# Attention in a two-layer hybrid block: the weighted values directly behind the next step's scores

## What is computed

```python
def block_attention(q, k, v):                      # 8 query heads, 2 key/value heads, HEAD_DIM 64
    qb = q.reshape(B, nb, Q_BLOCK, N_KV_HEADS, Q_PER_KV, HEAD_DIM).transpose(1, 0, 2, 3, 4, 5)
    def one_block(qblk):
        s = jnp.einsum('bqkgd,bskd->bkgqs', qblk, k, preferred_element_type=jnp.float32) * scale
        p = jax.nn.softmax(s, axis=-1).astype(v.dtype)
        return jnp.einsum('bkgqs,bskd->bqkgd', p, v)
```

## Time and profile before

| | us | share of the span |
|---|---|---|
| profiled execution | 1708.01 | |
| its span | 1706.2 | |
| TensorE matmul busy | 1616.7 | 95% |
| TensorE weight load busy | 1317.9 | 77% |
| VectorE (DVE) busy | 1014.3 | 59% |
| GpSimd (POOL) busy | 877.0 | 51% |
| ScalarE (ACT) busy | 624.3 | 37% |
| median of the three runs | 1710.27 | |

### The profile page before, as it was taken

How to read it: one execution, slowest core, us unless ns; L and a number is a source line. 1 busy time by engine, 2 the same in 40 slices (tenths; PEclk the granted TensorE clock), 3 DMA queues, 4 the chain that set the end, 5 groups by cost and what they waited for, 6 DMA issues and landing times. The chain is left out here.

```text
span 1706.2 us, 39559 instructions
## 1 busy us (share of the span) xinstructions
PE 1616.7 (95%) x17052; PEld 1317.9 (77%) x17052; DVE 1014.3 (59%) x1509; ACT 624.3 (37%) x1262; POOL 877.0 (51%) x763
## 2 busy tenths in 40 slices
PE   5999999989998899999999999998999889999998
PEld 4888999979997555546889999997899754554586
DVE  4563243828774778888338514382777478888911
ACT  5211231124444455555234223112444445545501
POOL 1001489039991477784230047911999338777432
PEclk9999999999999999999999999999999999999999
DMA  9455202210000000122320211221000000010422
GB/s 351 157 173 183 69 27 90 81 62 17 16 5 13 13 13 27 35 77 98 127 100 25 65 39 51 71 95 61 22 17 5 12 14 7 27 40 26 150 98 76
DMA packets 70124, 112.39 MB, mean 66 GB/s; under 512 B 10032, under 2 KB 42176, under 8 KB 69952
## 3 DMA queue, kind: packets, MB, share of 16 engines
q1 hardware_dynamic: 69200, 109.62, 19.3%
q10 hardware_dynamic: 752, 0.25, 0.1%
HBM read 90.30 MB, written 19.47 MB: 64 GB/s over the span
## 5 line engine op out<-in xcount | busy, mean ns | idle before, releaser
L1744 POOL TENSOR_TENSOR attn_accp<-attn_accp,attn_pr 128x1024 f32<-128x1024 f32 x110 | 266.8, 2426 | 48.5 <-ACT attn_pr L1821 43.3
L94 PE MATMUL ps<-in_h_hi,in_w_hi 128*128 128x384 f32 x672 | 226.8, 337 | 0.0
L96 PE MATMUL ps<-in_h_hi,in_w_lo 128*128 128x384 f32 x672 | 225.8, 336 | 0.0
L1821 ACT ACTIVATE attn_pr<-ps 128x512 f32<-128x512 f32 x292 | 158.9, 595 | 170.2 <-PE ps L1981 161.3
L2019 DVE TENSOR_REDUCE attn_mx<-ps 128x1 f32<-128x1152 f32 x128 | 172.3, 1354 | 74.3 <-PE ps L1936 73.5
L1980 PEld LDWEIGHTS ps<-attn_QH,attn_KH 128*128 128x128 f32 x292 | 55.5, 190 | 124.7 <-ACT attn_pr L1821 62.7
L1990 PE MATMUL ps<-attn_pr,z 128*64 128x512 f32 x520 | 140.6, 619 | 0.0
L1224 POOL TENSOR_TENSOR delta_ML<-delta_EK,local 128x256 f32<-128x256 f32 x180 | 130.7, 747 | 14.9 <-PE ps L1264 14.2
L1980 PE MATMUL ps<-attn_QH,attn_KH 128*128 128x512 f32 x292 | 131.8, 451 | 1.6 <-issue 1.4
L94 PEld LDWEIGHTS ps<-in_h_hi,in_w_hi 128*128 128x128 f32 x672 | 126.1, 188 | 5.0 <-issue 5.0
L96 PEld LDWEIGHTS ps<-in_h_hi,in_w_lo 128*128 128x128 f32 x672 | 126.1, 188 | 0.0
(11 more groups left out here) (313 smaller groups left out, 3853.9 us busy)
## 6 DMA issues: line engine op xcount, KB each, us to landing
in_w<-in_w_in SPq DMA_DIRECT2D x21, 1024.0 KB, 5.6
z<-in_w_mod SPq DMA_DIRECT2D x8, 2048.0 KB, 8.2
gates<-in_gate SPq DMA_DIRECT2D x48, 192.0 KB, 1.9
attn_gt<-gates SPq DMA_DIRECT2D x34, 256.0 KB, 2.6
z<-in_x_sample SPq DMA_DIRECT2D x16, 512.0 KB, 6.3
zz<-in_w_mod SPq DMA_DIRECT2D x8, 1024.0 KB, 10.1
out_w<-in_w_out SPq DMA_DIRECT2D x16, 512.0 KB, 6.6
out_y<-z SPq DMA_DIRECT2D x16, 512.0 KB, 2.9
```

Source lines behind the costliest of these rows:

```text
L94: nc.tensor.matmul(out, a_hi(i), b_hi(i), start=(i == 0), stop=False)
L96: last = nc.tensor.matmul(out, a_lo(i), b_hi(i), start=False, stop=(i == n - 1))
L1744: nc.gpsimd.tensor_tensor(acc, a, pr[:, n % 4], ALU.add).then_inc(pool_added, 1)
L1821: nc.scalar.activation(pr[:, n % 4, e], ps[:, e, :], ACT.Exp, scale=HD ** -0.5).then_inc(p_done, 1)
```

## The change

Inside an iteration the values move from the end to the place directly behind the scores. Nothing else is changed.

```diff
         for n, items in enumerate(steps):
             if n + 1 < len(ATTN_STEPS):
                 scores(n + 1)
+            weighted_values(n)
             for item in items:
                 work(item)
-            weighted_values(n)
         out["tensor"](pe, lambda: work(("sum", len(PAIRS) - 1)), nxt)
```

## The result

The changed kernel takes 1722.62 us, the median of 5 runs (1720.39 to 1727.70), against 1710.27 before (of five runs as well, 1708.93 to 1712.72). The ratio is 1.0072, with an interval of 1.0058 to 1.0086: slower by 9.9 to 14.7 us. In the profiled executions the span grew from 1706.2 to 1718.6, by 12.4.

The account below looks back on a forecast made before the run. TensorE, busy for 95% of the span, was taken to bound the kernel. The terms summed to +3.25 us per layer, +6.5 for two, on 1710.3: 1716.8 us, range 1712.5 to 1721, chance 0.70.

Parts of the forecast that it names:

- my third rival: Longer stillness before pair 2's scores drops the clock, up to 3 us more per layer: +12.5, 1723 us; chance 0.08.
- Waits for maxima: TensorE's waits for DVE, nearly all in steps 3 and 15, mostly remain: -0.2 us per layer, bounds -2.1 and 0.
- My first rival: The moved values fill TensorE's waits for maxima, winning 2.1 us per layer: 1709 us in total; chance 0.10.
- Lone sums: Five steps per layer where a maximum parts sum from values: 0.33 us lost each, +1.65, bounds 0 and 1.85.
- Row of pair 2: Values no longer lie under the row's DMA before pair 2's scores: +1.05 us per layer, bounds 0.7 and 1.2.
- Row of the last pair: One of two values blocks leaves the gap between row and scores: +0.45 us per layer, bounds 0 and 1.0.
- Turns and output turns: 13 steps per layer with transposes behind the maximum, next scores start late: +0.07 us each, +0.9, bounds 0 and 1.3.
- Row steps: Pairs 3 to 7: row, scores, values and maximum take 2.86 us, just covering 2.79 from row to scores: counted 0.
- Plain steps: 33 ordinary steps per layer with a maximum alone: -0.02 us each, -0.7 per layer, bounds -1.3 and +1.0.
- DVE's tail: Pair 7's sum comes 0.9 us later, so DVE's work behind it starts late: +0.1 per layer, bounds 0 and 0.9.
- The signs that I had named: Wrong if waits go, isolated sums cost nothing extra, or rows' DMA lands earlier than 2.2 us after issue.
- My second rival: Boundaries between kinds of matmul cost nothing, only the row's DMA shows: +2.8 us, 1713 us; chance 0.12.

Follow-up runs that it names:

- the ten instructions: Nine DVE scalings and pair 3's gate product replaced by one-input reciprocals, that work left out: 1712.97 us in the changed kernel, 1711.43 in the kernel before.

## Why the prediction was right in direction and wrong in size

**The step that failed** is in the first sentences of "the change part by part": everything an item produces comes about 1 us later against the scores, and "the order of DVE, ACT, POOL and SP stays". Both are true, and I took them to mean that DVE's chain moves as one block and costs nothing but in its tail. But POOL's additions hang on the exponentials, which follow the scores, and not on the items. So DVE's work moved by 1 us against POOL's. I used the row of 2.42 against 0.54 for one instruction at the end and didn't ask which other two-input DVE instructions would now meet an addition. The sum had no term for it. It is worth 5.13 us in layer 1 and 4.62 in layer 2 (the changed kernel with and without the ten instructions; in the old order the same ten are worth 0.3): 0.85 and 0.82 in step 7, 0.8 in step 8, 0.5 in step 18, 1.25 in step 38 of layer 2, and the 3.1 and 1.5 of steps 9 and 10. Of these last two a part is the clock's own: it can fall without the port's waits ahead of it, as the kernel with only step 8 changed shows. And the 3.1 is one execution's: with the sums first layer 1 lost 1.44 in the same two steps.

The Trainium skill (SBUF — State Buffer, section SBUF: two separate sides) says that a GpSimd operation, and a DVE operation with two SBUF inputs, take a shared port pair for their whole length, and the other "fully blocks". The trace agrees: 2.22 and 2.77 us where it was 0.51 and 0.67, and 0.54 for an instruction with one input at the same place.

**The clock** was my third rival, with 0.08, and "a single stillness between full steps" was the argument against it. The stillness was forecast well (1.6, it was 1.83), but it was not single: 0.82 and 0.30 of waits stood ahead of it. The kernel with only step 8 changed shows besides that 1.40 behind full steps can be enough. What it costs was forecast at up to 3 us per layer, and the run with unread matmuls measured 3.04 and 1.52. A chance of 0.08 was too small for something that had its nearest row in the same stage. That this rival's 1723 us is almost the measured time is luck: it stands on 3.25 us per layer from the other terms and 3 from the clock, and the kernels show 0.8 from the other terms and 4.9 from the port with the clock in it.

**Waits for maxima**: -0.2 per layer was forecast, -1.5 and -1.6 measured. I had also misread the row that this term stood on. The 2.8 us are not nearly all in steps 3 and 15: their longest wait stands ahead of step 0, where no values block moves. TensorE before, beside the 0.78 of step 3 in the earlier trace rows; the second row is step 15:

```profile
573.62 1.30 PE L1936 MATMUL ps<-attn_KH,attn_QH 128*128 128x384 f32 x3 [1.54 <-DVE attn_mx L2019]
...
623.90 0.77 PE L1936 MATMUL ps<-attn_KH,attn_QH 128*128 128x384 f32 x3 [0.43 <-DVE attn_mx L2019]
```

The argument that chains start in items was too coarse: step 3 went from 3.69 to 3.34 and step 15 from 3.37 to 3.02, and steps 37, 46 and 55, with a wait of 0.2 each, are 0.26 to 0.28 shorter in layer 1. My first rival was thus right for some seven tenths of its 2.1 us per layer; without it the loss would be 3 us larger.

**Lone sums**: forecast +1.65 per layer, measured 1.74 with the steps behind them. Right.

**Row of pair 2**: forecast +1.05, measured 0.78 to 0.90. Right within its bounds.

**Row of the last pair**: forecast +0.45, measured +0.32 and +0.29. The distance was 2.48 and not 2.79. The scores start 1.87 us behind the DMA's issue at 760.44 here, at other times later: step 62 took +1.04 in one of the other kernels, and 0.94 and 0.95 in two more. Less than 2.2 us behind the issue was a sign of being wrong that I had named. With the 0.19 that step 61 wins the term is only about +0.1.

**Turns and output turns**: forecast +0.9, measured about +0.1 in layer 1 and 0 in layer 2. The eight steps behind a turn or an output turn lose 0.62 and 0.57, and the steps with one win 0.07 and 0.11, but 0.46 and 0.45 of this belongs to the lone sums: it goes when the sums stand first.

**Row steps**, which I had counted at 0: -1.12 and -1.13 in the six of them, of which the steps behind 34, 43 and 52 give 0.30 and 0.27 back. In the old order the values started 0.21 us behind the last row (752.88 and 753.09); now the scores start 0.03 behind it (759.83 and 759.86). Why the row costs less there no run isolates.

**Plain steps**: forecast -0.7, measured 0.0. The 0.02 that I worked out for each is not there: 2.67 before and after. It was a small difference of two estimated boundaries, multiplied by 33, and it made the forecast 0.7 too low here.

**DVE's tail**: forecast +0.1, measured 0.

**The signs that I had named**: a step with a maximum alone takes 2.67 us, as it should, and one with a sum and a maximum 3.76 to 3.84 (3.85). The scores follow the row of pair 2 after 2.89 us (2.79) and that of the last pair after 2.48 (2.8). In steps 3 and 15 TensorE still waits, 0.64 and 0.30 us (0.5 to 0.8). The clock reads 1.00 up to 606 us and 0.51 from there.

The weight load behind values and transposes stays late, as forecast from the earlier trace rows: 0.81 us of idle PEld ahead of 724.51. My second rival, free boundaries, is out by the lone sums alone.

So without the ten instructions the change came to 0.8 us per layer where I had forecast 3.25. The waits took 1.2 to 1.3 off, the row steps 0.8, the turns 0.8 and the two rows' DMAs 0.4, and the plain steps put 0.7 on. The term that I had not written came to 4.9. The forecast of a slower kernel was right for the wrong sum, and partly by luck: with the ten instructions replaced in both orders, steps 1 to 70 differ by 1.11 and 1.03, about 2 us in all.

What stays open: why the scores behind a row's DMA start at times later than at others (0.7 us in step 62 of three stages, 1.0 in step 8 of one), and what decides the clock at a gap of 1.40.

## What to carry to other kernels

When a block moves, list for each engine what its instructions follow: those that follow the moved work and those that don't now stand otherwise against each other, though no engine's order has changed. Look for every DVE instruction with two SBUF inputs that comes within one POOL operation of its neighbour, and for what is queued behind it; a 0.5 us instruction whose result is not needed for long can hold up TensorE through the reduction behind it. The number of such meetings does not tell the cost: the old order had more of them and lost 0.3 us per layer by them. And look at what TensorE waited for in the steps ahead of a gap before calling the gap single. The cheapest gain of this case was to keep it busy with unread matmuls where it stood at half clock, 5 us.

## What the hardware showed that I had not expected

A DVE scaling with two inputs and 256 columns took 0.36 to 0.42 us where it met no addition of POOL, or one that began after it or was in its last 0.1 us. Where it started inside an addition, it ended 0.28 us behind that addition each time, in every trace of this case, and so took between 0.5 and 2.6 us. A reciprocal with a single input of 64 columns took 0.49 to 0.56 at the same places. It is not its size that spared it, since the scaling is the shorter of the two when it is alone; a one-input instruction of 256 columns was not tried there. The longest was a gate product of 512 columns, 2.77 against 0.67.

The grant of TensorE's clock, at one order and one gap (1.40 and 1.41 us behind full steps), was 0.51 in layer 1 and 1.00 in layer 2 of the same execution.

A sum with weights of 64 columns costs 0.35 us more where it stands alone than beside another block of its kind, and what the trace shows of it is the 0.81 us of idle weight loading ahead of the scores that follow.
